# Two-block attention and mixture-of-experts kernel: the order of exponential and copy on ScalarE in the first block's attention

## The reference

```
def one_block(qi):                       # 128 queries at a time
    s = jnp.einsum('bqhd,bkhd->bhqk', qi, k).astype(jnp.float32) * sm_scale
    p = jax.nn.softmax(s, axis=-1).astype(v.dtype)
    return jnp.einsum('bhqk,bkhd->bqhd', p, v)
```

## Time and profile before

| | |
|---|---|
| median of 3 runs | 1668.91 us (1666.24 to 1671.21) |
| profiled execution | 1666.24 us, its span 1664.4 us |
| PE busy | 1516.6 us, 91% of the span |
| DVE, ACT, POOL busy | 521.1, 453.3, 335.8 us |
| mean granted clock of PE | 0.958 of full speed |
| attention of pass 0 | from 156.2 to 190.4 us |
| attention of pass 1 | from 427.7 to 534.4 us |
| attention of pass 3 | from 801.5 to 909.0 us |

### The profile page before, as it was taken

One profiled execution on the slowest core, in us unless ns is written; L12 is line 12 of the kernel. 1 busy time (PEld: TensorE's weight loads), 2 busy tenths in 40 slices (PEclk: granted clock), 3 DMA queues, 4 the chain that ended last, 5 costly groups with the idle time before them and its releaser, 6 DMA issues.

```text
span 1664.4 us, 17320 instructions
## 1 busy us (share of the span) xinstructions
PE 1516.6 (91%) x6765; PEld 791.5 (48%) x6765; DVE 521.1 (31%) x1119; ACT 453.3 (27%) x886; POOL 335.8 (20%) x357
## 2 busy tenths in 40 slices
PE   3998889999799989999799989999999679999992
PEld 1676544444576544444576434455455433333330
DVE  0064310464443230465443121132043511121214
ACT  1233521222554232122554020042132201101101
POOL 1020000353100110345100000001622134333212
PEclk8899999999899999999799999999999789999996
DMA  8746022331020211211010121111320679999994
GB/s 293 259 165 233 4 98 102 126 104 48 1 105 2 92 51 51 76 51 50 1 53 1 51 101 50 51 51 51 105 102 1 235 268 393 375 414 391 400 410 181
DMA packets 85127, 232.98 MB, mean 140 GB/s; under 512 B 17025, under 2 KB 24967, under 8 KB 70840
## 3 DMA queue, kind: packets, MB, share of 16 engines
q1 hardware_dynamic: 69426, 201.93, 32.3%
q0 software_dynamic: 13824, 24.16, 4.0%
q10 hardware_dynamic: 1798, 5.80, 0.9%
HBM read 266.42 MB, written 16.80 MB: 170 GB/s over the span
## 4 chain that ended last, share of the span: by engine, by line
PE 87%; DMA 4%; ACT 3%; DVE 3%; issue 2%; POOL 0%; SPq 0%; POOLq 0%; ACTq 0%; DVEq 0%
PE PS L1733 18%; PE PS L2122 10%; PE PS L1891 8%; PE PS L1938 7%; PE PS L2143 5%; PE PS L1804 5%; PE PS L1714 4%; PE PS L1936 3%; PE PS L2031 3%; PE PS L1826 3%; PE PS L1814 2%; DMA RING<-in_w_mod_dram 2%; PE PS L1777 2%; PE PS L1973 1%; PE PS L2000 1%
## 5 line engine op out<-in xcount | busy, mean ns | idle before, releaser
L1733 PE MATMUL PS<-RH,RING 128*128 128x512 f32 (+1 forms) x864 | 315.4, 522 | 2.1 <-DMA RING<-in_w_in_dram 2.1
L1733 PEld LDWEIGHTS PS<-RH,RING 128*128 128x128 f32 x864 | 162.4, 190 | 147.8 <-issue 137.9
L1891 PE MATMUL PS<-RING,RY 128*128 128x512 f32 x320 | 139.4, 593 | 0.0
L2122 PE MATMUL PS<-RING,RM 128*64 128x512 f32 x384 | 116.1, 607 | 8.5 <-issue 5.6
L605 POOL TENSOR_SCALAR SMALL<-SMALL 128x1 f32<-128x1 f32 (+1 forms) x36 | 11.3, 314 | 537.8 <-ACT WS L839 258.2
L1295 DVE TENSOR_REDUCE SMALL<-PS 128x1 f32<-128x768 f32 (+1 forms) x80 | 68.0, 850 | 152.8 <-PE PS L1804 152.8
L1804 PE MATMUL PS<-RK,RH 96*128 96x256 f32 (+1 forms) x288 | 112.3, 512 | 3.3 <-ACT RH L947 3.3
L1938 PE MATMUL PS<-RH,RING 128*128 128x512 f32 x256 | 113.8, 593 | 0.0
L1254 DVE SCALAR_TENSOR_TENSOR RM<-RM,COL 128x512 f32<-128x512 f32 (+1 forms) x180 | 113.7, 701 | 0.1
L1891 PEld LDWEIGHTS PS<-RING,RY 128*128 128x128 f32 x320 | 60.1, 190 | 72.7 <-issue 72.7
L607 POOL TENSOR_TENSOR SMALL<-SMALL 128x1 f32<-128x1 f32 (+2 forms) x58 | 61.6, 1061 | 110.3 <-DVE SMALL L1220 107.3
(11 more groups left out here) (326 smaller groups left out, 2265.5 us busy)
## 6 DMA issues: line engine op xcount, KB each, us to landing
RING<-in_w_in_dram SPq DMA_DIRECT2D x18, 2048.0 KB, 8.0
RING<-in_w_mod_dram SPq DMA_DIRECT2D x12, 2048.0 KB, 8.6
RING<-in_w_expert_gate_dram SPq DMA_DIRECT2D x19, 1024.0 KB
RING<-in_w_expert_up_dram SPq DMA_DIRECT2D x19, 1024.0 KB
RING<-in_w_out_dram SPq DMA_DIRECT2D x8, 2048.0 KB, 8.9
RK<-in_w_expert_down_dram SPq DMA_DIRECT2D x8, 1024.0 KB
X<-in_w_expert_down_dram SPq DMA_DIRECT2D x8, 1024.0 KB
WS<-in_w_expert_down_dram SPq DMA_DIRECT2D x8, 1024.0 KB
```

The costliest lines, as they stand in the source:

```text
L1733: last = mm(o[:, 0:T], w[:, k, m * P:(m + 1) * P], HT[:, k, 0:T], start=(k == 0), stop=(k == 7))
L1891: last = mm(PS[:, j % 2, :], YT[:, k, t * P:(t + 1) * P], w[:, k, :], start=(k == 0), stop=(k == 7))
L2122: last = mm(PS[64 * z:64 * z + 64, n % 2, :], XGT[n % 2][:, k, 64 * z:64 * z + 64], free(GU[n % 3][z], [2048, 2], [1, DE], off=DE * k), st ...
```

## The change

In ACT's `attention`, the block with the copy of turn n-2 moves from ahead of the exponential of job n to behind it, within the same step. The waits go with their instructions; nothing is added or removed.

```
                     if n == 5:
                         conv_scale(i)
-                    if 2 <= n <= N + 1:
-                        k = n - 2
-                        act.wait_ge(p_t.sem, p_t.at(i, turn[(i, "T", k)]))
-                        if k >= 4:
-                            act.wait_ge(p_pv.sem, p_pv.at(i, (k - 4) // 2))
-                        A(PT[k % 4][:, 0:nk // P, :], free(PS[:, 4, :], [P, nk // P], [1, P]), ACT.Copy).then_inc(a_t.sem, 1)
                     if n < N:
                         q, h = divmod(n, 8)
                         act.wait_ge(v_mx.sem, v_mx.at(i, n))
...
                         A(PR[n % 2][:, 0:nk], src, ACT.Exp, bias=nmx[:, n % 4:n % 4 + 1], accum_out=DEN[:, q % 2, h:h + 1]).then_inc(a_e.sem, 1)
+                    if 2 <= n <= N + 1:
+                        k = n - 2
+                        act.wait_ge(p_t.sem, p_t.at(i, turn[(i, "T", k)]))
+                        if k >= 4:
+                            act.wait_ge(p_pv.sem, p_pv.at(i, (k - 4) // 2))
+                        A(PT[k % 4][:, 0:nk // P, :], free(PS[:, 4, :], [P, nk // P], [1, P]), ACT.Copy).then_inc(a_t.sem, 1)
                     if n == 7:
                         conv_silu(i)
```

## The result

The changed kernel takes 1713.3 us (median; 1711.94 to 1714.48) against 1669.64 us for the kernel before on the same chip, 1.0264 times as long, with a 95% interval of 1.0245 to 1.0283: 43.7 us slower. The forecast was 1705, 1697 to 1715, slower. The profiled execution took 1715.47 us, its span is 1713.6 us; lines 960 to 973 of the code are in the new order, so the exponential is L968 now and the copy L974.

The account below looks back on a forecast made before the run. PE, holding 87% of the chain, bounds the kernel. Passes 1 and 3 lose 16.9 us each (33.8), pass 0 3.4, together 37.2; on 1666.24 that gives 1703.4, with run spread taken as 1705, range 1697 to 1715.

Parts of the forecast that it names:

- the sequence that the prediction wrote down: Odd steps, long passes: maximum, exponential, copy, release to PE, 2.84 us in sum; even turn 1.09 late, 15 times per pass.
- The first case: The forecast as worked out, whole kernel, without more clock falls: 1699 to 1711 us, chance 0.86.
- clock falls more often: Rival: PE's new waits lower its clock more often; 1711 to 1730 us and beyond, chance 0.07.
- Even steps hidden: Copies held back in even steps cost odd turns nothing, covered by values' products and next scores with 0.9 us to spare.
- The denominators' turns: Steps 10, 18 and 26 of a long pass: each comes 0.59 us late, +1.77 per pass.
- The wait before `pointwise`: Step 8 of the long passes: PE's wait of 1.20 us shrinks to about 0.4.
- Turn 7 behind the table load: Long passes: it has 3.11 us and needs about 3.12, so it costs nothing, to a few hundredths.
- Nothing given back later: Work behind the attentions gives back none of the delay; the rival, given back in part, 1685 to 1699 us, had 0.04.
- Pass 0: Attention with 256 keys: five of seven even turns each 0.69 us late, 3.4 us in all, bounds 0 to 5.4.
- Turn 30 of the long passes: Behind the last exponential, already waiting for its copy: 1.23 us late instead of 1.09, +0.14 per pass.
- what `pointwise` takes back: Long passes, step 8: PE's existing wait there shrinks turn 6's delay from 1.09 to 0.22 us, -0.87 per pass.
- The rival "clock falls": Falls of about 1.7 us each; one in each tile of the long passes, 8 in all, gives 1719 us; chance 0.07.

Follow-up runs that it names:

- e3_odd: The new order only in odd steps, in all three passes, the kernel before's order in even steps; 1706.84 us, 1.0214 of the kernel before.
- e2_even: The new order only in even steps, in all three passes, the kernel before's order in odd steps; 1680.15 us, 1.0064 of the kernel before.
- e1_pass0: The new order only in pass 0, the kernel before's order in passes 1 and 3; 1675.79 us, 1.0038 of the kernel before.
- e7_fill: Changed kernel plus useless PE matmuls: 3 ahead of each even turn's wait in pass 0, 7 ahead of turn 30's in long passes; 1709.29 us.
- e4_last: Changed kernel, but with the copy first as before in the last step that has an exponential; 1707.56 us, 1.0221 of the kernel before.
- e5_pointwise: Kernel before with the first pointwise product of the convolution branch moved on PE from step 8 to the end of step 9; 1666.61 us, ratio 0.9984.
- e8_warm: Kernel before with useless matmuls (28, 5 and 5) where PE idles ahead of the attention of passes 1 and 3; 1662.07 us, ratio 0.9952.

## Why the prediction was right, and by how much it was off

*The place and the mechanism: right.* The changed kernel has the sequence that the prediction wrote down, with 2.83 us from the maximum's start to the turn where 2.84 was the sum. Two steps take 6.66 us (499.79 to 506.45, from turn 14 to turn 16) where 6.65 was forecast. e3_odd and e2_even put the cost on the odd steps, as forecast, against a cost of order in every step.

*The range held, but not by the case that it was built on.* The first case, without more falls of the clock, had a range of its own of 1699 to 1711, and 1713.3 lies outside of it. It lies among the 1711 to 1730 of "clock falls more often", and a fall of the clock was one of the signs by which the prediction was to be wrong. It did fall.

*Even steps hidden: right.* No odd turn waits in pass 1 of the changed kernel but turn 1, which has no products ahead of it.

*The denominators' turns: 0.67 each instead of 0.59* (489.70 and 509.23, set against the turns ahead of them, 2.11 and 2.78); the turns behind them are 0.72 late.

*The wait before `pointwise`: right.* It is 0.43 us; "about 0.4" was the forecast. *Turn 7 behind the table load: right.* It doesn't wait; the exponential starts 1.29 us after the load's start (470.35 and 471.64). The Trainium skill's figure of about 2.7 us with the drain ("ScalarE: Activation LUTs", section "What ACT_TABLE_LOAD costs") would have made the turn 1.4 late by the prediction's estimate, and the trace doesn't bear it out in this place.

*Nothing given back later: right.* The stretches between and behind the attentions differ by 0.9 us at most.

*The size: 37.2 forecast, 43.7 measured.* The term that was mis-sized is PE's clock, of which I had said that its falls would stay as they were, and given "clock falls more often" 0.07. In the changed kernel it fell for longer in pass 0 and newly at the end of the long passes:

- Pass 0: 3.4 forecast, 6.0 measured, and 6.0 again in e1_pass0. With the falls taken away (e7_fill) it is 3.1 longer than before from turn 0 on, near the forecast; the other 2.9 go with 15 us at half clock. The prediction read the waits of pass 0 wrongly. It took the 1.8 us before `pointwise` for the longest and said "the fall may as well go away, as its longest wait becomes shorter". The longest was turn 4's 2.02 us, and it grew to 2.53, while the one before `pointwise` shrank to 0.60. The sum of the waits behind the first scores grew from 6.4 to 8.7 us.
- Turn 30 of the long passes. I had its delay right (1.22 us measured, 1.23 forecast), but wrote it down as 1.23 for 1.09 and didn't add it to the 0.99 that PE waited there already. The sum, 2.21 us, is the longest wait of the pass, and PE's clock falls behind it. Turn 31 starts 1.46 later for it in pass 1 and 1.53 in pass 3. e4_last takes the wait away and the fall with it; e7_fill leaves nearly all of the delay, fills 1.73 us of it with matmuls, and the fall goes too. In pass 3 of e3_odd a wait of 2.21 us had no fall behind it, so such a wait can bring the fall and doesn't always.

The rest of the long passes: from turn 0 to turn 30 the changed kernel lost 17.5 us in each, where the sum says 16.9. The missing 0.6 is in two small terms for the most part: the denominators' turns (3 x 0.72 for 3 x 0.59) and what `pointwise` takes back (0.75 for 0.87). Ahead of turn 0, where no instruction had changed places, 0.6 more were lost in pass 1 and 1.0 won in pass 3, no more than that stretch differs by between runs whose code is the same there.

The rival "clock falls" had its price about right (1.7 us each, for about 1.5 at turn 30) and its place wrong: not one in each tile. The waits of 0.6 to 1.1 us in the long passes, fifteen of them in each, lowered nothing.

## What to carry to other kernels

Two instructions of one queue are to stand in the order in which their results are wanted, not in that in which they could start: ask which one the bottleneck engine asks for next, and what the one ahead of it waits for. An engine that has time in sum (27 of 44 us here) can still hold up the one that hasn't, once a short, urgent instruction stands behind a long one with a late condition. When a delay lands where there was a wait already, add the two before judging the clock: here waits of about 1 us lowered nothing, while 0.99 and a delay of 1.22 made 2.21, and half clock followed in three of four cases. And cut a trace where the unchanged part ends: the stretch ahead of turn 0 differed by up to 1.7 us between runs with the same code in it, and the rest of a long pass by 0.02.

## What I had not expected of the hardware

- After PE had been busy for 3.99 of 7.70 us, 15 us at 0.58 and 0.53 of full clock followed, although PE was busy for 5.14 of 6.00 and 8.92 of 9.20 us of them (part of that because the same matmuls take longer at half clock). e1_pass0 repeats it, and e7_fill, with matmuls in those waits, ran at 1.00 over the same part of the pass.
- Matmuls without a use in PE's waits pay here: with 28 + 5 + 5 of them ahead of each long pass, the stretch from 421 to 431 us ran at 1.00, and the kernel before became 8 us faster, 0.5%. The first scores and transposes ran at the 2.4 GHz level instead of the 1.2 GHz one.
- A wait of 2.21 us with the same work around it was followed by half clock three times and by full clock once (pass 3 of e3_odd, products at 1.53 us instead of 2.35 to 2.83).
- The first scores of an attention run at either clock with unchanged code: the first eight matmuls of a long pass took 5.37 us in pass 1 of the kernel before, 4.68 in e5_pointwise and 2.85 in e8_warm. This is where the lengths of whole passes wander.
